# Attention scores from two float32r matmuls over stacked high and low parts instead of one float32 matmul, and one product moved ahead of a normalisation

## The reference

```
q = rotary(rms_norm(q)); k = rotary(rms_norm(k))      # 16 query heads, 4 key heads, 64 wide
s = einsum('bnqhgd,bnjhd->bhgnqj', qb, kwin) * 64**-0.5   # blocks of 128 queries, windows of 3 blocks of keys
s = where(valid, s, -1e30)
m = maximum(max(s), sink)
p = exp(s - m); p = p / (sum(p) + exp(sink - m))
o = einsum('bhgnqj,bnjhd->bnqhgd', p, vwin) * silu(gate)
```

## Time and profile before

| | |
|---|---|
| median of 3 runs | 3012.84 us (3011.98 to 3013.04) |
| the profiled execution | 3012.62 us |
| its span, first to last instruction | 3010.8 us |
| PE busy | 2977.7 us, 99% of the span |
| VectorE busy | 1754.0 us, 58% |
| ScalarE busy | 1169.8 us, 39% |
| GpSimd busy | 1410.7 us, 47% |
| mean granted TensorE clock | 0.998 |
| attention steps of layer 0 | from 588.25 us to 704.67 us |

### The profile page before, as it was taken

How to read it: one execution, slowest core, us unless ns; L and a number is a source line. 1 busy time by engine, 2 the same in 40 slices (tenths; PEclk the granted TensorE clock), 3 DMA queues, 4 the chain that set the end, 5 groups by cost and what they waited for, 6 DMA issues and landing times.

```text
span 3010.8 us, 41665 instructions
## 1 busy us (share of the span) xinstructions
PE 2977.7 (99%) x14092; PEld 2429.5 (81%) x14092; DVE 1754.0 (58%) x2661; ACT 1169.8 (39%) x1751; POOL 1410.7 (47%) x1040
## 2 busy tenths in 40 slices
PE   8999999999999999999999999999999999999998
PEld 6888888867888888888887788878888888788886
DVE  7986677775524598568687644367773243611214
ACT  4233333464332424333336533236553333422223
POOL 5443443455555443443344555543443545454544
PEclk9999999999999999999999999999999999999999
DMA  4222222212233322222221232321222323222222
GB/s 151 98 72 76 90 84 79 83 43 92 93 102 100 123 94 84 84 84 76 78 91 50 73 103 98 98 91 64 77 77 91 107 86 101 91 98 97 92 97 91
DMA packets 73272, 267.90 MB, mean 89 GB/s; under 512 B 8128, under 2 KB 9024, under 8 KB 72768
## 3 DMA queue, kind: packets, MB, share of 16 engines
q1 hardware_dynamic: 70560, 254.84, 25.3%
q10 hardware_dynamic: 2592, 11.46, 1.0%
HBM read 262.07 MB, written 4.19 MB: 88 GB/s over the span
## 4 chain that ended last, share of the span: by engine, by line
PE 85%; issue 7%; POOL 5%; DVE 2%; ACT 0%; DVEq 0%; POOLq 0%; ACTq 0%
PE gem L375 19%; PE gem L376 19%; PE gem L377 19%; POOL wlo L308 5%; PE gem L775 2%; PE gem L777 2%; PE gem L776 2%; PE gem L497 2%; PE gem L498 2%; PE gem L496 2%; PE gem L616 2%; PE gem L639 1%; PE xp L675 1%; PE gem L618 1%; PE gem L617 1%
## 5 line engine op out<-in xcount | busy, mean ns | idle before, releaser
L308 POOL TENSOR_TENSOR wlo<-raw,whi 128x512 fp32r<-128x512 f32 x956 | 1315.2, 1397 | 1536.5 <-ACT whi L937 1536.4
L937 ACT ACTIVATE whi<-raw 128x1024 fp32r<-128x1024 f32 x478 | 504.6, 1056 | 680.4 <-PE gem L377 508.9
L375 PE MATMUL gem<-zhi,whi 128*128 128x512 f32 x1680 | 655.9, 390 | 0.3 <-DVE zlo L1561 0.3
L377 PE MATMUL gem<-zhi,wlo 128*128 128x512 f32 x1680 | 653.9, 389 | 0.0
L376 PE MATMUL gem<-zlo,whi 128*128 128x512 f32 x1680 | 653.6, 389 | 0.0
L375 PE MATMUL gem<-hhi,whi 128*128 128x512 f32 x1296 | 505.2, 390 | 0.0
L377 PE MATMUL gem<-hhi,wlo 128*128 128x512 f32 x1296 | 504.3, 389 | 0.0
L376 PE MATMUL gem<-hlo,whi 128*128 128x512 f32 x1296 | 504.2, 389 | 0.0
L375 PEld LDWEIGHTS gem<-zhi,whi 128*128 128x128 f32 x1680 | 315.4, 188 | 66.8 <-DVE zlo L1561 0.8
L377 PEld LDWEIGHTS gem<-zhi,wlo 128*128 128x128 f32 x1680 | 315.3, 188 | 65.9
L376 PEld LDWEIGHTS gem<-zlo,whi 128*128 128x128 f32 x1680 | 315.4, 188 | 65.2 <-issue 0.2
(11 more groups left out here) (390 smaller groups left out, 4246.8 us busy)
## 6 DMA issues: line engine op xcount, KB each, us to landing
raw<-in_slabs SPq DMA_DIRECT2D x478, 512.0 KB, 3.5
U<-in_x SPq DMA_DIRECT2D x4, 512.0 KB, 7.9
U<-in_x ACTq DMA_DIRECT2D x1, 2048.0 KB, 10.2
xsave<-U ACTq DMA_DIRECT2D x1, 2048.0 KB, 8.2
U<-xsave ACTq DMA_DIRECT2D x1, 2048.0 KB, 8.4
out_y<-yr SPq DMA_DIRECT2D x8, 256.0 KB, 2.2
tab<-in_tab_ret ACTq DMA_DIRECT2D x2, 512.0 KB, 8.2
tab<-in_tab_att ACTq DMA_DIRECT2D x2, 512.0 KB, 3.6
```

Of the source, the lines that this page charges most:

```text
L308: part = pool.tensor_tensor(wlo[:, k % 4, c], raw[:, k % 2, c], whi[:, k % 4, c].bitcast(f32), O.subtract)
L375: pe.matmul(o, wh, hi, start=(n == 0), stop=False)
L377: mm = pe.matmul(o, wl, hi, start=False, stop=(n == len(terms) - 1))
L937: act.activation(whi[:, k % 4, :], raw[:, k % 2, :], A.Copy).then_inc(hi_done, 1)
```

## The change

1. **Parts.** For each pair a tile `x` of 128 partitions is made for each head: the head's 64 query rows rounded to float32r in its own half (ACT, `queries_high`), and the remainder of the same rows in the other half (DVE, `queries_low`). For each of the four key heads there are two tiles: `kh`, the rounded key rows in both halves (ACT, `keys_high`), and `kl`, the remainder in the head's own half and zeros in the other (DVE, `keys_low`). One matmul of `x` with `kh` then gives high x high plus low x high, and one of `x` with `kl` adds high x low. They reuse tiles that are free at that time (`Z[L]`, and `QR[0]` to `QR[3]` for the second pair of key heads).
2. **Scores.** `qk(t)` has two float32r matmuls on 128 partitions in place of each float32 matmul on 64.
3. **Where the parts are made.** Keys 0 and 1 and queries 0 to 3 ahead of or behind step 0; queries 4 to 7 in steps 2, 5, 8, 11 (ACT) and 3, 6, 9, 12 (DVE); keys 2 and 3 in steps 4 and 7 (ACT) and 5 and 8 (DVE).
4. **Order.** DVE's `gate(p)` stands between `maxes(t)` and `normalise(t-1)` instead of behind `normalise(t-1)`.

```
+        def key_parts(L, i):
+            if i < 2:
+                return tuple(t[:, 6 + i, :] for t in Z[L])
+            return tuple(Ur[:, a + (i - 2) * T:a + (i - 1) * T] for a in (U_A + 2 * T, U_C))
+        def query_parts(L, p):
+            return tuple(t[:, (p + 4) % 6, :] for t in Z[L])
+        def head_rows(hf):
+            return slice(hf * 64, hf * 64 + 64), slice(64 - hf * 64, 128 - hf * 64)
...
# PE, qk(t)
-                    pe.wait_ge(a_rope, L * 10 + 3 + p)
+                    pe.wait_ge(x_ready, L * 8 + p + 1)
+                    pe.wait_ge(k_ready, L * 4 + 2 * pr + 2)
...
-                            rows = slice(hf * 64, hf * 64 + 64)
-                            mm = pe.matmul(scores_of(t, hf)[:, cols], QR[p][rows, n * P:(n + 1) * P],
-                                           KA[rows, pr, lo * P:hi * P], start=True, stop=True)
+                            o, x = scores_of(t, hf)[:, cols], query_parts(L, p)[hf][:, n * P:(n + 1) * P]
+                            kh, kl = key_parts(L, 2 * pr + hf)
+                            pe.matmul(o, x, kh[:, lo * P:hi * P], start=True, stop=False)
+                            mm = pe.matmul(o, x, kl[:, lo * P:hi * P], start=False, stop=True)
...
# ACT
+                def keys_high(i):
+                    src, kh = KA[head_rows(i % 2)[0], i // 2, :], key_parts(L, i)[0]
+                    act.activation(kh[0:64, :], src, A.Copy)
+                    act.activation(kh[64:P, :], src, A.Copy).then_inc(k_high, 1)
+                def queries_high(p):
+                    act.wait_ge(a_rope, L * 10 + 3 + p)
+                    for hf in range(2):
+                        r = head_rows(hf)[0]
+                        last = act.activation(query_parts(L, p)[hf][r, :], QR[p][r, :], A.Copy)
+                    last.then_inc(x_high, 1)
...
                     if t < 24:
                         exps(t)
+                    if t in (4, 7):
+                        act.wait_ge(x_ready, L * 8 + 4)
+                        keys_high(t // 3 + 1)
+                    if t in (2, 5, 8, 11):
+                        queries_high(p + 4)
...
# DVE
+                def keys_low(i):
+                    r, other = head_rows(i % 2)
+                    kh, kl = key_parts(L, i)
+                    dve.wait_ge(k_high, L * 4 + i + 1)
+                    dve.memset(kl[other, :].bitcast(f32), 0.0)
+                    tt(kl[r, :], KA[r, i // 2, :], kh[r, :].bitcast(f32), O.subtract).then_inc(k_ready, 1)
+                def queries_low(p):
+                    dve.wait_ge(x_high, L * 8 + p + 1)
+                    for hf in range(2):
+                        r, other = head_rows(hf)
+                        x = query_parts(L, p)[hf]
+                        last = tt(x[other, :], QR[p][r, :], x[r, :].bitcast(f32), O.subtract)
+                    last.then_inc(x_ready, 1)
...
                 maxes(0)
+                queries_low(3)
                 a_rotated(8)
...
                     maxes(t)
-                    normalise(t - 1)
                     if c == 2:
                         gate(p)
+                    normalise(t - 1)
+                    if t in (5, 8):
+                        keys_low(t // 3 + 1)
+                    if t in (3, 6, 9, 12):
+                        queries_low(p + 3)
                     if c == 0 and p >= 2:
                         gated_head(p - 2)
```

More of the change, by code:

```diff
@@ L235, in build @@
         osq, ossq, ovar, orstd = (sem(n) for n in ("osq", "ossq", "ovar", "orstd"))
+        k_high, k_ready, x_high, x_ready = sem("k_high"), sem("k_ready"), sem("x_high"), sem("x_ready")
         a_sq, a_low, a_ssq, a_rs, a_kn, a_rope = (sem(n) for n in (
@@ L1015, in layer @@
                 g0, u0 = L * LAYER_GROUPS, L * LAYER_USES
-                zhi = Z[L][0]
+                zhi, zlo = Z[L]
                 act.wait_ge(consts, 7)
@@ L1197, in layer @@
                         a_square(k + 4)
+                    if k == 0:
+                        act.wait_ge(a_rope, L * 10 + 1)
+                        keys_high(0)
+                        keys_high(1)
+                    else:
+                        queries_high(k - 1)
                 G, u = g0 + ATT[0], u0 + ATT[1]
@@ L1203, in layer @@
                 a_square(6)
+                queries_high(2)
+                queries_high(3)
                 def turned_p(t):
@@ L1964, in layer @@
                     add_out(G + 3, u + 3, (k,))
+                    if k == 1:
+                        keys_low(0)
+                        keys_low(1)
+                    elif k > 1:
+                        queries_low(k - 2)
                 ts(NSK, vec[:, C_SINK:C_SINK + 16], -1.0, None, O.mult)
@@ L1967, in layer @@
                 a_rotated(6)
+                queries_low(2)
                 a_rotated(7)
```

## The result

| | before | after |
|---|---|---|
| median of 18 runs each | 3011.67 us (3010.59 to 3013.04) | 3018.51 us (3016.56 to 3019.97) |
| ratio after to before | | 1.0022 (95% interval 1.0015 to 1.0029) |
| profiled execution | 3012.62 us | 3019.58 us |
| its span | 3010.8 us | 3017.8 us |
| `qk(0)` to `qk(23)`, layer 0 | 110.00 us | 113.39 us |

The changed kernel is 6.8 us slower, 2.5 us above the forecast and inside both ranges. That is 0.22%, at the very edge of the 0.2% up to which the prediction called the two kernels the same. The last two rows (starts in the list in order of time, subtracted: 588.25 to 698.25 us before, 588.82 to 702.21 us after in layer 0) hold 6.95 us, which is the whole difference of the profiled executions. So only the attention steps need reading.

What follows compares the result with a forecast made beforehand. PE, busy 99%, bounds the kernel; the question was DVE's room. a_pv(9) 4.2 us late less 2.6 us saved gives 1.6 us a layer, 3.2 us in both: 3016 us on 3012.6; range 3004 to 3026, likeliest case 3010 to 3019.

Steps and rivals of the forecast that it cites:

- PE's saving: Score matmuls: 0.34 us less in 16 steps and 0.08 us in 8, 6.1 us a layer, 12.2 us in both.
- Weight loads of 188 ns: Rival at the score matmuls: loads can't overlap, saving falls to 1.4 us a layer, 3019.4 us; chance 0.10.
- (1): Ahead of slab 5: queries_low(3) delays gate(0), PE's next slab 1.1 us late, stall from 0.69 to about 2.6 us.
- (2): From gate(0) to gated_head(2): DVE needs 50.0 us instead of 45.2, so a_pv(9) starts 4.2 us late.
- the term of the waits: DVE's new wait for the tanh at gates 1 and 2, 1.45 us each, 2.9 us; none at gate 3.
- which a DVE that is late doesn't have: From gate(0) to gated_head(2): DVE's earlier waits, 7.7 us, were taken off its time.
- (3): After step 12: nothing added, DVE still waits, PE keeps its saving of 2.6 us a layer.
- Hidden after all: Rival: DVE's additions in the attention steps are hidden, 4.0 us saved a layer, 3005 us; chance 0.20.
- DVE against POOL: Rival: new subtractions take 0.914 us each and two a layer are held by POOL, 3022 us; chance 0.24.
- The gate's order: At the gates: normalise(1), 0.3 us, moves behind gate(0), and DVE newly waits for the tanh at gates 1 and 2.

Runs made afterwards that it cites:

- gate_back: Changed kernel with DVE's gate(p) put back behind normalise(t-1), nothing else changed: 3013.42 us, ratio to the kernel before 1.0006.
- keys_early: Changed kernel with ACT's keys_high in steps 3 and 6 instead of 4 and 7: 3015.71 us, ratio to the kernel before 1.0012.
- best: Changed kernel with gate behind normalise, query parts 4 to 7 later, queries_low(3) behind gate(0), key parts earlier, gated_head ahead of the parts: 3001.69 us.
- q_late: Changed kernel with parts of queries 4 to 7 later: ACT in steps 8, 11, 14, 17, DVE in 10, 13, 16, 19: 3005.79 us.
- no_lows: Changed kernel without DVE's queries_low of pairs 4 to 7 and keys_low of key heads 2 and 3: 3004.36 us.
- gate_only: Kernel before with only the gate moved ahead of normalise(t-1), float32 scores kept: 3011.37 us, ratio 0.9999.
- q3_late: Changed kernel with queries_low(3) moved from between maxes(0) and a_rotated(8) to step 2, behind gate(0): 3020.15 us.
- best_twice: The `best` kernel with one pair of DVE subtractions, queries_low(6) in step 16, done twice: 3004.52 us.
- best_gate_ahead: The `best` kernel with gate(p) ahead of normalise(t-1), as in the changed kernel: 3002.12 us.
- gh_first: Changed kernel with gated_head(p-2) ahead of queries_low in steps 6, 9 and 12: 3015.78 us, ratio to the kernel before 1.0013.

## Why the prediction was nearly right

**PE's saving.** The prices held: 384 columns 0.17 to 0.18 us apart (0.177 estimated), 256 columns 0.12 (0.124). Across the kernels, stage less PE's waits in layer 0 (where no stretch ran at half clock) is 103.9 us in `gate_back`, `keys_early` and `best`, 103.8 in `q_late` and 103.7 in `no_lows`; in the kernel before and `gate_only` it is 109.3. That is 5.4 us for 23 steps where the forecast has 5.7 (15 x 0.34 + 8 x 0.08). Weight loads of 188 ns and more did not bind; that rival is excluded.

**(1) `queries_low(3)` ahead of `gate(0)`.** The stall is 2.35 us in layer 0 and 2.27 in layer 1 (about 2.6 forecast). That it was no loss by itself shows in `q3_late`.

**(2) From `gate(0)` to `gated_head(2)`: the step that failed.** 51.75 us in place of 50.0, `a_pv(9)` 5.7 us late in place of 4.2. The prices of the added steps were right: `queries_low` 0.69 + 0.98 us (1.7 forecast), `keys_low` about 1.15 us (1.25). What was too small is the term of the waits, 2.9 us: gates 1 and 2 waited 1.86 and 1.90 us (1.45 each forecast), gate 3 waited 1.08 us (none forecast), and scores were waited for 1.4 us (none forecast), 6.2 us in all. The rest came out 1.6 us lower, and that was luck: a small DVE step like that of the earlier trace rows stood over a microsecond beside POOL's weight subtraction three times in this stretch before (1.16, 1.17, 1.17 us) and once after (1.17 us), a shift that the forecast did not count.

The sentence "which a DVE that is late doesn't have" was the mistake, and what it missed is in the main the clock. Of the 3.3 us above the forecast, 2.5 us (gate 3 and the scores) stand behind stalls where PE then ran at half clock, a state that the forecast does not contain: DVE made PE stall, PE came out of the stall slow, and DVE waited for its scores and its transposes. The other 0.9 us stands at gates 1 and 2. In ACT's chain ahead of gate 2 the two copies of `keys_high` took 1.30 us (1.1 forecast), and the whole chain to the tanh took 5.2 us (4.85 forecast). The first of the two stretches at half clock cost little: layer 1 had none behind its first stall, and its way from `gate(0)` to `gated_head(2)` is 51.50 us.

**(3) The tail** saved 2.3 us from `a_pv(9)` to `qk(23)` (44.14 us before, 41.85 after), 2.6 forecast. Together 5.7 - 2.3 = 3.4 us a layer in place of 1.6. By PE's side of layer 0 it is 5.8 us more of waiting and 3.0 us of half clock, less 5.4 us saved. The forecast's range held; its term for the waits was half of what came.

**The rivals.** *Hidden after all:* false for this order, but `q_late` and `best` show that it needs only other steps. *DVE against POOL:* the 0.98 us are real and were in the price. In `q_late` the four later pairs lasted 0.69 us, so 0.29 us each came of the place; hits of over 1 us on a new subtraction, which this rival needs, came only in `best_twice`. The Trainium skill ("GPSIMD Engine Reference", 1. Specifications) says that GpSimd's SBUF interfaces are shared with VectorE and contended by DVE instructions with two SBUF inputs. The rows agree in part: the second subtraction lasts 0.98 in place of 0.69 us, and POOL's pair of probabilities beside it 2.96 us, against 2.46 us in `best` where no subtraction overlaps it. But the first subtraction of the pair, which started 0.07 us ahead of POOL's, lasted 0.69 us, and that of `keys_low` at 622.67 us lasted 0.68 us beside a pair of 2.47 us. So not every overlap costs.

**The gate's order** was forecast at 0.3 us of moved work and the wait for the tanh. In the changed kernel it costs 5.1 us in both layers (`gate_back`), a part of it by the clock, in kernels with slack on DVE nothing (`gate_only`, `best_gate_ahead`). The two parts of the change are not additive.

## What to carry to other kernels

A microsecond of work on an engine off the critical path costs nothing, or about a microsecond, by where it stands: list the engine's waits over each stretch, and put new work into the stretch that has them, as late as its reader allows. Don't take an engine's waits as used up because it has come late: they came back here where PE left a stall at half clock, and where ACT's own chain ran long. And don't read a wait that got shorter as time that was won: ask whether the instruction behind it came earlier. In `gh_first` (gate 1) and `keys_early` (gate 2) it did not, since another delay stood in its place. Before an instruction is moved, look up every reader of its semaphore; a count that stood for "all done" can hide one.

## What the hardware showed that I had not expected

Behind some stalls TensorE's granted clock fell from 2.4 to 1.2 GHz for a few microseconds, which the kernel before shows nowhere in its attention steps. The changed kernel, behind the stall of 2.88 us that ended at 644.78 us (stretch, busy us, instructions, granted clock, DMA share, GB/s):

```profile
646.00:650.00 4.00, 4.00 (x12) 0.58 0.00 0
650.00:654.00 4.00, 4.00 (x36) 1.00 0.28 78
```

and ordinary 512-column matmuls behind the first stall, 0.43 us apart in place of 0.23:

```profile
609.26 0.63 PE L632 MATMUL gem<-hlo,whi 128*128 128x512 f32 x1
609.69 0.63 PE L633 MATMUL gem<-hhi,wlo 128*128 128x512 f32 x1
```

Over the attention steps of all fourteen traces, PE had 41 waits of 0.5 to 1.9 us and none was followed by a lower clock; of 32 waits of 2.0 us and longer 19 were. The same wait of 2.3 us ahead of slab 5 was followed by it in some executions and layers and not in others (`q_late`: not in layer 0, yes in layer 1). What it costs is what is left of a stage when the waits and the 103.85 us of undisturbed work are taken off: 3.0 us for the two in layer 0 of the changed kernel (113.39 - 6.5 - 103.85) and 1.4 us for the one in layer 1 of `q_late` (108.15 - 2.9 - 103.85), so about 1.5 us each (1.4 to 1.7 us in seven of the eight layers with one, 2.1 us in the eighth). Behind the first stall, where DVE set the pace, taking it away gave nothing back (`q3_late`, and the changed kernel's layer 1 against its layer 0). Behind the second it kept DVE waiting, as the table above shows. What decides between a stall of 2 us with and one without it stays open.
